# Feature tiles of x's high and low parts placed 1028 bytes apart in SBUF instead of 1024

## What is computed

```python
def first_block(x, ...):
    for i in range(2):
        hn = rmsnorm(h, mix_norm_g[i])
        mix = gated_deltanet(hn, dn_w_in, ..., dn_w_out) if i == 0 else moba_layer(hn, mb_w_in, mb_w_out)
        h = h + mix
        h = h + squared_relu_mlp(rmsnorm(h, mlp_norm_g[i]), mlp_w_up[i], mlp_w_down[i])
    return rmsnorm(h, final_norm_g)

def second_block(x, mem, ...):
    h = _rms_norm(x, norm_mix_pre)
    ... = split(h @ w_in)                      # four branches, then gates = sigmoid(h @ w_gate)
    x = x + _rms_norm(sum(gates * proj) @ w_out)
    x = x + cross attention(x, mem)
    u = _dwconv_causal(_rms_norm(x) @ w_up, ffn_dw) + ffn_dw_b
    x = x + _rms_norm((silu(u_g) * u_v) @ w_down)
```

## Time and profile before

| | |
|---|---|
| device time, median of 3 runs (lowest, highest) | 1250.72 us (1250.34, 1251.28) |
| span of the profiled execution, first to last instruction | 1249.1 us |
| TensorE busy with matmuls | 1220.7 us, 98% of the span |
| TensorE loading weights | 1106.9 us, 89% |
| VectorE / ScalarE / GpSimd busy | 871.6 / 700.5 / 56.3 us |
| mean granted TensorE clock, share of full speed | 0.998 |
| DMA, mean rate over the span | 169 GB/s |

### The profile page before, as it was taken

How to read it: one execution, slowest core, us unless ns; L and a number is a source line. 1 busy time by engine, 2 the same in 40 slices (tenths; PEclk the granted TensorE clock), 3 DMA queues, 4 the chain that set the end, 5 groups by cost and what they waited for, 6 DMA issues and landing times.

```text
span 1249.1 us, 21521 instructions
## 1 busy us (share of the span) xinstructions
PE 1220.7 (98%) x8583; PEld 1106.9 (89%) x8583; DVE 871.6 (70%) x1252; ACT 700.5 (56%) x1016; POOL 56.3 (5%) x102
## 2 busy tenths in 40 slices
PE   8999989999999999999999999999999999999997
PEld 7999988888888998888888999999999977888886
DVE  5888567666666656666656589998656577778876
ACT  4984555555455554554554564656454456666663
POOL 5010020000000001000000000000000010000000
PEclk9999999999999999999999999999999999999999
DMA  7671134666554654565555565354546534555561
GB/s 223 197 203 68 38 122 150 222 214 202 186 184 151 203 165 141 166 211 180 184 185 167 172 210 184 118 162 145 179 150 203 186 107 147 174 194 190 201 201 68
DMA packets 160340, 210.80 MB, mean 169 GB/s; under 512 B 5542, under 2 KB 143220, under 8 KB 160261
## 3 DMA queue, kind: packets, MB, share of 16 engines
q1 hardware_dynamic: 157315, 202.77, 50.6%
q0 software_dynamic: 1904, 6.85, 1.4%
q10 hardware_dynamic: 1042, 0.07, 0.1%
HBM read 208.62 MB, written 1.05 MB: 168 GB/s over the span
## 4 chain that ended last, share of the span: by engine, by line
PE 79%; DVE 10%; ACT 4%; issue 2%; DMA 2%; SPq 1%; POOL 1%; DVEq 0%; POOLq 0%; ACTq 0%
PE bank L369 16%; PE bank L373 16%; PE bank L372 16%; PE bank L454 15%; PE bank L450 8%; DVE wlo L305 3%; ACT whi L297 2%; PE bank L1425 2%; DMA raw<-in_dn_w_in 1%; DVE common L2582 1%; PE bank L2003 1%; PE bank L1445 1%; ACT common L753 1%; SPq L3388 1%; PE bank L2095 1%
## 5 line engine op out<-in xcount | busy, mean ns | idle before, releaser
L305 DVE TENSOR_TENSOR wlo<-raw,whi 128x2048 fp32r<-128x2048 f32 x190 | 434.9, 2291 | 203.6 <-ACT whi L297 203.3
L297 ACT ACTIVATE whi<-raw 128x2048 fp32r<-128x2048 f32 x190 | 363.3, 1913 | 145.4 <-PE bank L369 43.5
L369 PE MATMUL bank<-xparts,whi 128*128 128x256 f32 x912 | 262.5, 288 | 0.4 <-DVE common L2764 0.4
L373 PE MATMUL bank<-xparts,wlo 128*128 128x256 f32 x912 | 258.7, 284 | 0.0
L372 PE MATMUL bank<-xparts,whi 128*128 128x256 f32 x912 | 258.6, 284 | 0.0
L454 PE MATMUL bank<-xparts,whi 128*128 128x512 f32 x832 | 208.0, 392 | 0.0
L369 PEld LDWEIGHTS bank<-xparts,whi 128*128 128x128 f32 x912 | 175.5, 192 | 2.8 <-issue 2.1
L372 PEld LDWEIGHTS bank<-xparts,whi 128*128 128x128 f32 x912 | 175.6, 192 | 0.6 <-issue 0.5
L373 PEld LDWEIGHTS bank<-xparts,wlo 128*128 128x128 f32 x912 | 175.5, 192 | 0.0
L454 PEld LDWEIGHTS bank<-xparts,whi 128*128 128x128 f32 x832 | 149.8, 189 | 26.9
L369 PE MATMUL bank<-whi,hhi 128*128 128x512 f32 x392 | 153.1, 391 | 3.8 <-DVE hlo L1061 2.3
(11 more groups left out here) (391 smaller groups left out, 1706.2 us busy)
## 6 DMA issues: line engine op xcount, KB each, us to landing
raw<-in_mlp_w_up SPq DMA_DIRECT2D x32, 1024.0 KB, 5.5
raw<-in_mlp_w_down SPq DMA_DIRECT2D x32, 1024.0 KB, 5.1
raw<-in_w_in SPq DMA_DIRECT2D x22, 1024.0 KB, 5.3
raw<-in_w_up SPq DMA_DIRECT2D x22, 1024.0 KB, 5.2
raw<-in_w_gate SPq DMA_DIRECT2D x16, 1024.0 KB, 5.5
raw<-in_dn_w_in SPq DMA_DIRECT2D x15, 1024.0 KB, 5.8
raw<-in_mb_w_in SPq DMA_DIRECT2D x12, 1024.0 KB, 5.2
raw<-in_w_down SPq DMA_DIRECT2D x11, 1024.0 KB, 4.9
```

The costliest lines, as they stand in the source:

```text
L297: nc.scalar.activation(whi[:, s, :], raw[:, r, :], ACT.Copy).then_inc(hi_ready, 1)
L305: nc.vector.tensor_tensor(wlo[:, s, :], raw[:, V % RAW, :], f32(whi[:, s, :]), ALU.subtract).then_inc(lo_ready, 1)
L369: ins = pe.matmul(o, shi, mhi, start=first, stop=False, skip_group_check=True)
L373: return pe.matmul(o, slo, mhi, start=False, stop=last, skip_group_check=True)
```

## The change

The rows of `xparts` get one more float that nobody uses, so a tile starts 1028 bytes behind the one before it instead of 1024. Every read and write goes through the same views.

```diff
         whi = sb("whi", [P, RING, UNIT], F32R)
         wlo = sb("wlo", [P, RING, UNIT], F32R)
-        xparts = sb("xparts", [P, 2, KT, T], F32R)
+        xrows = sb("xparts", [P, 2, KT, T + 1], F32R)
+        xparts = xrows[:, :, :, 0:T]
         xhi, xlo = xparts[:, 0], xparts[:, 1]
```

## The result

The changed kernel takes 1260.7 us (median of 4 runs, 1258.6 to 1261.1) beside 1250.5 us for the kernel before. The ratio is 1.0068, interval 1.0055 to 1.0081: slower by 0.7%, about 8.5 us (7 to 10 by the interval; the two medians are 10.2 us apart). The forecast was 1244.3 us and faster.

The account below looks back on a forecast made before the run. TensorE's matmul pace was taken to bound the kernel. Terms of -7.5, -0.7 and +0.3 us, with the others at nothing, summed to -7.9 us, times 0.81 -6.4 us: 1250.7 to 1244.3 us, range 1236 to 1268 us.

Parts of the forecast that it names:

- What bounds the kernel: Whole kernel: TensorE has matmuls in flight for 98% of the span, so a matmul's cost is seen at the end.
- The share of 0.81: Part of TensorE's summed change taken to reach the end: chain 79% on PE, PE busy 98%; -7.9 us becomes -6.4 us.
- x moving, 256 wide: mm3 and L450: 3412 matmuls with shifted tiles gain 2.2 ns each, -7.5 us, bounds -11.9 to +23.2 us.
- L454: In wide_features, 832 matmuls with x moving, 2 x 256 wide: 0 taken, between -2.9 and +5.7 us.
- x stationary: Matmuls with x stationary: -0.7 us with 256 columns moving, +0.3 us with 512.
- Everything behind xparts: Buffers behind xparts move 64 bytes; weights against hhi assumed to keep 226.5 ns, else +8 us on 1176 matmuls.
- the likeliest case: Whole kernel: faster as the terms sum, 1244.3 us, own range 1236 to 1248, chance 0.42.
- No change: Matmuls reading x: the start within 32 bytes doesn't count and x keeps its pace, 1250.7 us; chance 0.20.
- the coarse dependence: Matmul operands: only coarser differences in start affect pace; if low tiles alone gain, -2.0 us, about 1248.7 us.
- The slower one: Shifted moving x costs 1 to 6.8 ns more on 4244 matmuls; 1262 us at half, 1274 at the whole; chance 0.25.
- The steep one: Reads of x starting off 8 bytes run at half rate, +96 ns per narrow matmul, 1461 us; chance 0.13.

Follow-up runs that it names:

- the tail alone: Kernel before with 64 unused bytes behind xparts, x itself as before, so only what lies behind moves: 1258.4 us, ratio 1.0049.
- x at 32: Kernel before with all of xparts 32 bytes later, tiles 1024 bytes apart: ratio 1.0009; with everything behind on its old place within 512 bytes, 0.9966.
- the spacing alone: Kernel before with tiles 1028 bytes apart and 448 more unused bytes behind, so hhi and bhi keep their old place within 512 bytes: ratio 1.0019.
- 64 or 192: Kernel before with xparts 64 or 192 bytes past the weights' place modulo 256, the rest on its old place: 1245.6 us (0.9944) and 1243.5 us (0.9941).

## Why the prediction was wrong

**What bounds the kernel.** Right. The change moved TensorE's pace, and 9.5 us of pace at full clock came out as 8.5 us of time (7 to 10), that of the tail alone, 8.4 us, as 6. The share of 0.81 that reaches the end lies within what both leave open, and isn't tested more closely than that.

**x moving, 256 wide: -7.5 us.** Measured -3.5, and -2.5 at full clock. The sign was right, the size a half to a third of the forecast, and the row of `bhi` at 32 was a good price for x at 32 (-8.7 and -1.7 us with x at 32). What it left out was named as the way to be wrong: no row starts off 16 bytes, and three in four tiles of the change do. With a spacing of 1040, all starts on 16, the same two entries are -7.9 us at full clock; the rest is most likely the price of starts off 16, with the reserve made above.

**L454: 0 taken, -2.9 to +5.7 given.** Measured +3.8, inside its bounds: +2.2 already with all starts on 16 (spacing of 1040), the rest likely from starts off it.

**x stationary: -0.4.** Measured -0.4.

**Everything behind xparts: taken at nothing. This step failed.** I had seen that all aligned rows had multiples of 128 on both sides, priced `hhi` at +8 us should the 64 bytes count, and still assumed that the place within 64 bytes is all that counts. It measured +7.4 us, and +1.1 on `bhi` that I hadn't priced. The tail alone gives 0.49 of the 0.68%. From the -7.9 us forecast to the +8.5 us measured, by the same means, it is 8.5 us of the miss (with small entries on `bhi`), L454 3.8 and the narrow x matmuls 4.0. With this one term taken from its upper end, the sum would have been -7.9 + 8 us, no change, and the likeliest case no longer faster. No row of before spoke for the assumption, and two buffers at distance 32 already showed that distance matters; nothing favoured a finer dependence over a coarser one. It should have been a rival with a chance.

**The rivals.** *No change*: wrong, but the coarse dependence that it rested on exists. *The slower one* gave 1262 us, near the measured time, by another mechanism: x was to lose 3.4 ns on every read. It lost on L454 only, and `hhi`, which that rival didn't touch, lost most. *The steep one* is refuted: a start 4 bytes off costs 3 ns on 120 at x's every tile, not 96.

**The range** held the time (1236 to 1268), but by luck: its upper end came from the slower rival, whose mechanism isn't the one that acted. The sign was wrong.

## What to carry to other kernels

Where matmuls in fp32r bound a kernel, the distance of the two operands' starts modulo 256 bytes is a knob, worth 0.5% either way in this kernel, free of instructions: read the pace (start to start) of like matmuls in buffers at different places, and keep tiles on multiples of 16 bytes (starts 4 bytes off lost on every x matmul here). A buffer that grows moves all that is declared behind it, so a change of one size can change the distance of every tensor behind it; pad it to 256 bytes, or test the shift by itself, as here with 64 bytes that nobody reads. And a price that is known only from aligned neighbours belongs into the range with its sign open.

## What the runs showed of the hardware that wasn't expected

- The pace of back-to-back fp32r matmuls at the granted 2.4 GHz depends on the distance between moving and stationary operand modulo 256 bytes: 113.3 to 120.0 ns for 256 columns, 226.9 to 234.0 for 512 columns of weights, best at 0 there and at 192 for the narrow ones. Moving both operands together changes nothing (0.9995). Whether the stationary operand that matters is this matmul's own or the next one's, loaded meanwhile, isn't told apart: both lie in the same buffers here. Why the distance counts wasn't found.
- At one distance the pace can settle at two values (113.3 and 117.8 ns) for the same instructions.
- A moving operand 4 bytes off a multiple of 16 costs 3 ns at 256 columns, 10 ns at 2 x 256 (239.7).
- The pace of a matmul also depends on something other than its own distance: with x at 32, 64 or 192 the untouched `hhi` matmuls are at 227.6 to 228.5 instead of 226.9 ns.
- The granted clock of TensorE drops from 2.4 to 1.2 GHz in some executions more often than in others: 3.4 us in all in the profiled one of the kernel before (beside the very end), none with the tail alone, 10.2 us with the spacing alone. The time goes with it: in one series of the same kernel before, 1250.8 us at a mean clock of 0.998 (5 executions), 1252.5 at 0.997 (12), 1254.2 at 0.995 (4). A difference of 1 to 3 us between two variants is easily mistaken for one of pace.
